# Expert numbers of a head on VectorE alone: subtraction of the place and a minimum of magnitudes in place of a one-hot and products on GpSimd

## The reference

```
q = (xf @ w_q).reshape(T, PEER_HEADS, PEER_DKEY)
s1 = jnp.einsum('thd,nd->thn', q[..., :PEER_HALF], k1).astype(F32)
s2 = jnp.einsum('thd,nd->thn', q[..., PEER_HALF:], k2).astype(F32)
v1, i1 = lax.top_k(s1, PEER_TOPK)
v2, i2 = lax.top_k(s2, PEER_TOPK)
cand = (v1[..., :, None] + v2[..., None, :]).reshape(T, PEER_HEADS, PEER_TOPK * PEER_TOPK)
sc, pidx = lax.top_k(cand, PEER_TOPK)
e1 = jnp.take_along_axis(i1, pidx // PEER_TOPK, axis=-1)
e2 = jnp.take_along_axis(i2, pidx % PEER_TOPK, axis=-1)
expert = (e1 * PEER_NKEYS + e2).reshape(T, n_sel)
...
act = jax.nn.gelu(jnp.einsum('td,tkd->tk', xb, u_tab[eb]))
return jnp.einsum('tk,tkd->td', gb * act, v_tab[eb])
```

## Time and profile before

| | |
|---|---|
| three runs | 3512.60, 3522.31, 3525.66 us; median 3522.31 |
| profiled execution | span 3512.3 us; no time beside the span is listed for it, the fastest run is 0.3 us above it |
| busy | TensorE 3196.7 us (91%), VectorE 2751.0 (78%), GpSimd 1947.2 (55%), ScalarE 1387.6 (40%) |
| products on GpSimd (line 1550) | 68 instructions, 130.7 us |
| gathers on GpSimd (line 1571) | 1072 into `rows` for dot products, 1416.5 us |
| dot products on VectorE (line 1773) | 1072 on `rows`, 1326.4 us |
| first one-hot table, last product | starts at 495.7 us and at 2740.4 us |

### The profile page before, as it was taken

How to read it: one execution, slowest core, us unless ns; L and a number is a source line. 1 busy time by engine, 2 the same in 40 slices (tenths; PEclk the granted TensorE clock), 3 DMA queues, 4 the chain that set the end, 5 groups by cost and what they waited for, 6 DMA issues and landing times.

```text
span 3512.3 us, 57824 instructions
## 1 busy us (share of the span) xinstructions
PE 3196.7 (91%) x18338; PEld 2567.2 (73%) x18338; DVE 2751.0 (78%) x5867; ACT 1387.6 (40%) x3099; POOL 1947.2 (55%) x1504
## 2 busy tenths in 40 slices
PE   7999999999999989988999999999989999998655
PEld 4777766666666668767878888888877888877554
DVE  3333357998988887889899999999999887666776
ACT  4444311333332221587555555555555565000110
POOL 0000013565577763345776776767767775676776
PEclk9999999999999999999999999999999999999899
DMA  8444455788899998778999999999999999999998
GB/s 268 150 149 150 139 165 165 254 264 285 260 323 328 322 340 306 248 252 304 396 390 396 392 387 397 371 365 396 387 346 392 375 409 404 386 410 408 407 408 345
DMA packets 429325, 1127.33 MB, mean 321 GB/s; under 512 B 41968, under 2 KB 166256, under 8 KB 429168
## 3 DMA queue, kind: packets, MB, share of 16 engines
q0 software_dynamic: 204800, 745.10, 56.7%
q1 hardware_dynamic: 219600, 370.51, 29.6%
q10 hardware_dynamic: 4768, 9.96, 0.8%
HBM read 1098.82 MB, written 26.62 MB: 320 GB/s over the span
## 4 chain that ended last, share of the span: by engine, by line
DVE 18%; issue 15%; DMA 14%; PE 12%; POOL 5%; ACT 1%; POOLq 0%; DVEq 0%; ACTq 0%; SPq 0%
DMA rows<-in_peer_u,eidx 10%; DVE rows L1773 7%; PE vacc L2377 6%; POOL rows L1571 3%; DMA W<-in_peer_v,eidx 2%; DVE oh1w L1854 2%; PE vacc L2291 2%; DMA rows<-in_peer_v,eidx 2%; PE scat L2311 2%; POOL W L1571 1%; DVE oh L1849 1%; DVE eidx L1667 1%; DVE htok L1783 1%; PE scat L2364 1%; DVE ti L1718 1%
## 5 line engine op out<-in xcount | busy, mean ns | idle before, releaser
L1571 POOL DMA_INDIRECT rows<-in_peer_u,eidx x1072 | 1416.5, 1321 | 846.7 <-DVE dots L1773 501.1
L2377 PE MATMUL vacc<-W,vbuf 128*128 (+1 forms) x6144 | 1425.6, 387 | 32.6 <-DMA vbuf<-in_peer_v 23.6
L1773 DVE CUSTOM_DVE_ANT_0 rows<-rows,htok 128x1024 f32<-128x1024 f32 x1072 | 1326.4, 1264 | 157.7 <-DMA rows<-in_peer_u,eidx 149.1
L2377 PEld LDWEIGHTS vacc<-W,vbuf 128*128 128x128 f32 x6144 | 1156.8, 192 | 183.2 <-issue 34.0
L2111 ACT ACTIVATE oh<-iota,e2s 128x128 bf16<-128x128 f32 x1536 | 486.5, 391 | 17.3 <-DVE wpart L1825 10.0
L928 PE MATMUL vacc<-W 128*128 128x384 f32 x1280 | 430.8, 493 | 1.2 <-ACTq L805 1.2
L1550 POOL TENSOR_TENSOR hot<-hot,ccid 128x864 f32<-128x864 bf16 x68 | 130.7, 1927 | 530.1 <-DVE hot L1758 528.8
L928 PEld LDWEIGHTS vacc<-W 128*128 128x128 f32 x1280 | 241.8, 192 | 168.7 <-issue 6.8
L2118 ACT ACTIVATE W<-scat 128x256 f32 (+1 forms) x320 | 122.9, 384 | 563.5 <-PE scat L2364 560.3
L2114 ACT ACTIVATE oh<-oh,ones 128x512 bf16<-128x512 bf16 x384 | 277.2, 722 | 12.5
L1854 DVE TENSOR_TENSOR oh1w<-oh,wpart 128x768 bf16<-128x768 bf16 x384 | 241.8, 630 | 44.3 <-PE scat L2364 24.4
(11 more groups left out here) (346 smaller groups left out, 3281.0 us busy)
## 6 DMA issues: line engine op xcount, KB each, us to landing
vbuf<-in_peer_v SPq DMA_DIRECT2D x384, 512.0 KB, 6.7
W<-in_w_in SPq DMA_DIRECT2D x80, 512.0 KB, 6.6
W<-in_wq SPq DMA_DIRECT2D x64, 512.0 KB, 4.3
vbuf<-in_w_ada SPq DMA_DIRECT2D x9, 2048.0 KB, 8.0
rows<-in_peer_u,eidx POOLq DMA_INDIRECT x1072, 7.3
W<-in_w_in SPq DMA_DIRECT2D x16, 1024.0 KB, 6.3
W<-in_w_ada SPq DMA_DIRECT2D x3, 2048.0 KB, 15.9
W<-in_w_out SPq DMA_DIRECT2D x12, 512.0 KB, 6.6
```

The costliest lines, as they stand in the source:

```text
L1571: g.indirect_dma_start(row_of[s], None, table[:, :], bass.IndirectOffsetOnAxis(ap=picked, axis=0)).then_inc(landed[s], 16)
L1773: v.tensor_tensor_reduce(row_of[s], row_of[s], htok[:, home, :], 1.0, 0.0, ALU.mult, ALU.add, dots_of(t)[:, c:c + 1]).then_inc(used, 1)
L2377: mm = pe.matmul(vacc[:, k, :], vbuf[:, s, k * P:(k + 1) * P], W[:, e1, :].rearrange("p o t -> p (o t)"), start=(clear and s == 0 and k % ...
```

## The change

The expert numbers of a unit are found by VectorE alone. A place is added to both parts of an expert number, so that candidate number p carries p x 32768 on top of its expert number (`ID_STEP`; the places are a new constant of 2 x 16 numbers, loaded beside the others). Piece 14 multiplies the positions of the 16 best by 32768, in fp32. Piece 15 subtracts that from all 54 candidates, for each of the 16 (1728 fp32 elements for a full unit): the candidate at that position leaves its bare expert number, below 16384, and every other one a magnitude above 16384. The minimum of magnitudes along the 54 is the expert number. The one-hot table, the products and their two semaphores are gone; `ids` runs in piece 15 and no longer in the next unit.

```diff
+ID_STEP = 2 * NKEY * NKEY
...
+    place = np.stack([np.arange(TOPK), np.arange(TOPK)])
+    for i0, ni, nj, p0 in STAIRS:
+        place[0, i0:i0 + ni] = p0 + nj * np.arange(ni)
+    place = place * ID_STEP
...
-        bp, bpf = sb(ctx, "bp", [P, 2, TOPK], U32), sb(ctx, "bpf", [P, 2, TOPK], BF16)
+        bp, bpf = sb(ctx, "bp", [P, 2, TOPK], U32), sb(ctx, "bpf", [P, 2, TOPK])
+        place = sb(ctx, "place", [P, 2, TOPK])
...
-                def products(m, t):
-
-                    g.wait_ge(pos_ready, m + 1)
-                    shp = [P, TOPK // 2, 2, NCAND]
-                    h4 = hot[:, t, :, :].rearrange("p (a b) n -> p a b n", b=2)
-                    g.tensor_tensor(h4, hotb[:, t].rearrange("p a n b -> p a b n"), cid[:, t, :].unsqueeze(1).unsqueeze(1).broadcast_to(shp), ALU.mult).then_inc(hot_ready, 1)
...
-                def ids(m):
-
-                    G, h, nt = unit(m)
-                    v.wait_ge(hot_ready, products_done(m))
-                    with nc.allow_low_precision(reason="one number of each row is not zero, and it is an integer"):
-                        v.tensor_reduce(eidx[:, picks_slot(G), 0:nt, h * TOPK:(h + 1) * TOPK], hot[:, 0:nt, :, :], AX, ALU.add).then_inc(idx_ready, 1)
+                def ids(G, h, nt):
+
+                    shp = [P, nt, TOPK, NCAND]
+                    dl_(v.tensor_tensor(hot[:, 0:nt, :, :], bc(cid[:, 0:nt, :], 2, shp), bc(bpf[:, 0:nt, :], 3, shp), ALU.subtract))
+                    with nc.allow_low_precision(reason="the smallest distance of each row is a whole number below 2**14"):
+                        v.tensor_reduce(eidx[:, picks_slot(G), 0:nt, h * TOPK:(h + 1) * TOPK], hot[:, 0:nt, :, :], AX, ALU.min, apply_absolute_value=True).then_inc(idx_ready, 1)
...
-                        if p == 8 and m and m != H + NSU:
-                            ids(m - 1)
...
-                        v.tensor_scalar(tvf[:, 0, 1, :, :], ti[:, 0, :, :], float(NKEY), None, ALU.mult)
-                        dl_(v.tensor_copy(tvf[:, 1, 1, :, :], ti[:, 1, :, :]))
+                        v.scalar_tensor_tensor(tvf[:, 0, 1, :, :], ti[:, 0, :, :], float(NKEY), bc(place[:, 0, :], 1, [P, 2, TOPK]), ALU.mult, ALU.add)
+                        dl_(v.tensor_tensor(tvf[:, 1, 1, :, :], ti[:, 1, :, :], bc(place[:, 1, :], 1, [P, 2, TOPK]), ALU.add))
...
-                        v.tensor_copy(bpf[:, 0:nt, :], bp[:, 0:nt, :]).then_inc(tk, 1)
+                        v.tensor_scalar(bpf[:, 0:nt, :], bp[:, 0:nt, :], float(ID_STEP), None, ALU.mult).then_inc(tk, 1)
...
-                        shp = [P, nt, TOPK // 2, NCAND, 2]
-                        v.tensor_tensor(hotb[:, 0:nt], iota4[:, 0:NCAND, :].unsqueeze(1).unsqueeze(1).broadcast_to(shp),
-                                        bc(bpf[:, 0:nt, :].rearrange("p t (a b) -> p t a b", b=2), 3, shp), ALU.is_equal).then_inc(pos_ready, 1)
+                        ids(G, h, nt)
```

More of the change, by code:

```diff
@@ L217, in tables @@
         "iota": np.broadcast_to(np.arange(P)[None], (P, P)),
+        "place": np.broadcast_to(place[None], (P, 2, TOPK)),
     }
@@ L482, in _ @@
                 for dst, src in ((rope_c, "rope_c"), (rope_s, "rope_s"), (dmask, "dmask"), (smask, "smask"), (xi, "xi"),
-                                 (zeta, "zeta"), (szeta, "szeta"), (gch, "gch"), (h0, "h0"), (c0, "c0"), (iota, "iota")):
+                                 (zeta, "zeta"), (szeta, "szeta"), (gch, "gch"), (h0, "h0"), (c0, "c0"), (iota, "iota"), (place, "place")):
                     sp.dma_start(dst[:], I[src]).then_inc(small_in, 16)
@@ L1268, in _ @@
             def _(act):
-                act.wait_ge(small_in, 240)
+                act.wait_ge(small_in, 256)
                 for k in range(KC):
@@ L1302, in _ @@
                 v.memset(zA.las[:, :, 0:1], 0.0)
-                v.wait_ge(small_in, 240)
+                v.wait_ge(small_in, 256)
                 dl_.flat()
@@ L1332, in program @@
         scaled2, q_ps, qh_ready, s_ps, s_ready, tr_ready, tr_free = (sem(n) for n in ("scaled2", "q_ps", "qh_ready", "s_ps", "s_ready", "tr_ready", "tr_free"))
-        tk, dk, pos_ready, hot_ready, idx_ready, max_ready, exp_ready = (sem(n) for n in ("tk", "dk", "pos_ready", "hot_ready", "idx_ready", "max_ready", "exp_ready"))
+        tk, dk, idx_ready, max_ready, exp_ready = (sem(n) for n in ("tk", "dk", "idx_ready", "max_ready", "exp_ready"))
         landed = [sem(f"landed{i}") for i in range(VW)]
@@ L1389, in spilled @@
             return m - H if m < H + NSU else m - H - 2
-        def products_done(m):
-            return sum(unit(x)[2] for x in range(m + 1))
         def softmax_at(g):
@@ L1595, in reload_at @@
                     return min(read[m - 2] + 8, done[m - 1] + 1)
[L1597 to L1604, removed]
                 for n in range(NJOB):
@@ L1613, in _ @@
                             reload(m + 1)
-                        for x in range(unit(m)[2]):
-                            if n == product_at(m, x):
-                                products(m, x)
             @block.vector
@@ L1951, in _ @@
                     if half:
-                        ids(H + NSU - 1)
                         v.wait_ge(idx_ready, H + NSU)
@@ L2317, in scores @@
                     if G < NGRP:
-                        pe.wait_ge(small_in, 256)
+                        pe.wait_ge(small_in, 272)
                         pe.wait_ge(qh_ready, 2 * (G * H + h) + 2)
```

4 lines of the change are left out of this document (removed).

## The result

Four runs of the changed kernel have a median of 3495.8 us (3494.2 to 3496.3), four runs of the kernel before beside them 3524.0 us (3512.6 to 3526.2): a ratio of 0.9926, with an interval from 0.991 to 0.9942. The change is faster by 28 us; 3492 was predicted, and 30 us. Timed twice more, the changed kernel had 3495.9 us (ratio 0.9936 [0.992, 0.9953]) and 3493.4 us (0.9939 [0.9925, 0.9953]).

What follows compares the result with a forecast made beforehand. Between 1657 and 2742 us TensorE sets the pace and VectorE, held up by GpSimd products, is late at single steps. Gains of 20, 6 and 4 us make 30 off the median 3522: 3492 us, range 3467 to 3513.

Steps and rivals of the forecast that it cites:

- Products removed: VectorE's dots and scalings no longer held by GpSimd products: 45.4 us back between 1657 and 2742, 12.8 and 10.3 earlier.
- GpSimd counted at nothing: Two GpSimd instructions of about 1.9 us leave each full unit, between the gathers; GpSimd has room, so no gain counted.
- Subtraction: At each unit's end on VectorE: 1.96 us, +0.91 over the comparison in 32 full units, 30.9 us in all.
- Minimum: Minimum of magnitudes replacing the sum on VectorE: 1.944 us as before, no gain; a second pass would cost 70 us.
- The lump: Subtraction and minimum together, 3.9 us in one place on VectorE, covered by its lead of two batches: counted as nothing.
- Share that arrives: Between 1657 and 2742 us, 20 of VectorE's 30.8 us arrive, because gathers come due sooner at a denser pace.
- the long stretch: 1657 to 2742 us, where TensorE runs over the value table while VectorE still works off the heads' units.
- the proportional share: Gather waits between 1657 and 2742 us grow in proportion to gain g: g = 30.8 - 49 x g/89, so 20 us.
- The two stretches ahead of it: 500 to 1310 us, mixing later tokens, 4 us gained; 1310 to 1657 us, queries and scores, 6 us gained.
- Gather ring: Rival: gather slots, reused after six dots, limit VectorE; the 20 us vanish, the other 10 become 6: 3516; chance 0.15.
- Everything arrives: Rival: gathers start earlier and gather waits don't grow; some 55 us gained, 3467; chance 0.10.
- The longer subtraction shuts the gathers out: Rival: gathers meeting the subtraction are held up to 1.96 us, the new pair costs 30.9 us: 3543; chance 0.05 with the fourth.

Runs made afterwards that it cites:

- the lump apart: Changed kernel with the minimum moved back to the next unit's piece 8, subtraction left at the unit's end: 3492.4 us, then 3488.3 us.
- nothing put in: Kernel before without the GpSimd products, its sum replaced by a minimum over bare candidates, so other numbers come out: 3480.4 us, ratio 0.9881.
- the 66 products: Changed kernel with 66 unused GpSimd products put back at their old places, each waiting for the unit's expert numbers: 3557.0 us, ratio 1.0096.
- the 56 late products: Changed kernel with 56 unused GpSimd products of two tables, placed two and more gathers later: 3560.8 us, ratio 1.012.
- the 56 copies: Changed kernel with 56 unused one-input GpSimd copies of 864 elements, placed two and more gathers later: 3514.1 us, ratio 0.9989.

## Why the prediction was right

**Products removed.** Right in its mechanism, and the runs show it: with fills in their place 34 of 40 us are won. VectorE's rows over the whole span give 1072 x (1.264 - 1.219) = 48 us for the dots and 384 x (0.630 - 0.557) = 28 for the scaling, 76 where the stretches summed to 68.5. Of these 40.5 us arrive, a bit more than half, GpSimd's own 3 to 9 us among them.

**GpSimd counted at nothing.** Nearly right for the removal, 3 to 9 us. It does not hold the other way round: GpSimd's time added to the changed kernel cost 20 and 30 us. The reason given, "GpSimd has room there (766.4 of 1085 us busy)", would have been wrong for that by its whole size; that the gathers right behind were due would explain it, but no run shows it.

**Subtraction.** 1.953 us for 1.96, 30.6 us in all for 30.9. **Minimum**: 1.953 for 1.944, one pass.

**The lump.** This is the mis-sized step. "I count nothing either way" is 3 to 5 us. VectorE's two batches of lead cover the lump in most units, but not at the two group ends, where the evacuation is due behind the last unit's subtraction and minimum: 7.0 us became 13.1. It is about what the forecast lacks (3496 for 3492, 28 us for 30), but that it alone explains the rest isn't shown, since other terms err by as much.

**Share that arrives.** For the long stretch 20 us were forecast of 30.8. From the first step to the last 14.6 arrive (12.8 and 13.5 in the other two traces), with the lump apart 1581.8 - (3213.8 - 1647.8) = 15.8 and 1581.8 - (3207.9 - 1649.0) = 22.9. So the share came out lower than forecast; the lump took a part of the rest, between 3.0 and 9.4 us by the two pairs of traces. Whether the proportional share is right without it isn't settled: of 45.4 us with nothing put in 23.9 arrived, where it gives 29. The two stretches ahead of it were to give 4 + 6 us: TensorE's output mixing begins 4.3 us earlier (1317.5 for 1321.8) and the first step 10.0 (8.3 and 13.3 in the other two traces). That the whole comes within 2 us of the forecast 30 is in part luck: the traces give 14.6 + 10.0 us less 6.5 behind the last step, and the other 10 us of the measured 28 can't be given to any term of the sum.

**The rivals.** *Gather ring*: gather waits rose by 19.7 us in the long stretch, more than the 10 expected and less than the 30 that would have made the rival hold. *Everything arrives*: no. *The longer subtraction shuts the gathers out*: it does, at a small price. The changed kernel at one unit's end, timeline of VectorE and GpSimd (start, duration, instruction, idle before):

```profile
1974.03 1.95 DVE L1649 TENSOR_TENSOR hot<-ccid,bpf 128x1728 f32<-128x1728 f32 x1
1974.70 2.10 POOL L1566 DMA_INDIRECT rows<-in_peer_u,eidx  x1 [1.71 <-issue]
1976.02 1.95 DVE L1651 TENSOR_REDUCE eidx<-hot 128x32 uint32<-128x1728 f32 x1
```

The gather that is issued under the subtraction ends at 1976.80, 0.8 us behind it. The 29 gathers that start between 1640 and 2740 us and overlap a subtraction take 1.79 us in the mean, the other 505 take 1.31; before, the 26 under a comparison took 1.26. So 29 x 0.53 = 15 us of GpSimd's time go to the longer instruction. How much of that arrives in the kernel's time no run separates; the time, 15 us over the kernel without products, leaves room for little, since VectorE's own 30.6 us are in it too. A gather under the minimum alone, which has one input, takes 1.05 us (19 of them, in the kernel with the minimum apart). The rule in the Trainium skill, "SBUF — State Buffer", section "SBUF: two separate sides", is that of VectorE's instruction with two SBUF inputs and a GpSimd instruction that reads SBUF the one that starts first gets the shared pair of ports for its whole length, and the other one waits. The runs agree with it on three points: products and copies stretch the dots to 3.5 and 2.5 us, fills that read nothing leave them at 1.3 at most, and gathers wait out the subtraction and not the minimum. On who comes first they agree only in part: dots that start 0.7 to 0.9 us ahead of a product run through, and the product takes 2.04 to 2.22 us instead of 1.88; but by the recorded starts dots that start up to 0.57 us ahead of it are held.

## What to carry to other kernels

The instructions on GpSimd that read SBUF here, products and copies, were not beside VectorE but in its way: before counting such a one as hidden, look at the longest, not the mean, of VectorE's instructions with two inputs, and price it by what they lose. Where a change joins two instructions into one row, look for the places at which the engine's lead has run out (the ends of groups here), because there the added row arrived nearly whole (7.0, 13.1 and 16.6 us of wait at two places with 1.05, 3.9 and 5.9 us in a row). Busy share says nothing of the price of time added between transfers that are issued in order: it has to be tried at its place.

## What the runs showed of the hardware

- A held instruction does nearly all of its work behind the GpSimd instruction that holds it. In the kernel before and the three runs with products or copies added, all 95 dots above 1.35 us end 1.08 or 1.09 us behind it and all 84 scalings above 0.65 us end 0.41 to 0.43 us behind it, for GpSimd instructions of 0.91 to 2.4 us.
- A GpSimd fill leaves dots and scalings alone, but not everything: in the kernel before with fills, the cast of `wpart` with one input, 0.23 us by itself, took 1.39 and 1.09 us in the two places where a fill ran, and ended 0.08 us behind it.
- VectorE lost 0.60 to 0.68 of the length of the GpSimd instructions tried here that read SBUF. Dots and scalings together, per instruction, beside its median length: before 76/68 = 1.12 us beside 1.88 (0.60); the 66 products 82/66 = 1.25 beside 2.03 (0.61); the 56 late products 84/56 = 1.49 beside 2.20 (0.68); the 56 copies 35/56 = 0.62 beside 1.02 (0.61).
- A minimum of magnitudes over 1728 fp32 elements takes 1.953 us, as a subtraction of as many with both operands repeated does.
- A gather that overlaps a subtraction of 1.95 us on VectorE takes up to 2.5 us, where 0.93 is its shortest.
